# Expert layers: the second block's remainder of the down weights is subtracted on GpSimd instead of VectorE

## The chip, the cores and the metric

The kernel runs on one core of a Trainium2 chip. The metric is the device time of one execution in microseconds. The time before is the median of 3 runs; one more execution was taken with the hardware profiler.

## What is computed

One inference step of a small diffusion backbone with two layers over 640 tokens (512 latent, 128 context), model width 1024. Each layer has an attention mixer (differential attention in layer 0, latent attention in layer 1) and then the channel mixer with which this change deals: PEER, a retrieval among 16384 experts, of which each token and head takes 16.

```
def peer(h, wq, sub_keys, u, v):        # per block xb of 128 tokens
    q = (xb @ wq).reshape(TOK_BLOCK, PEER_HEADS, 2, PEER_HALF)
    s = einsum('thcd,hcnd->thcn', q, sub_keys)
    top_s, top_i = lax.top_k(s, PEER_TOPK)
    ...
    g = jax.nn.softmax(fs, axis=-1)
    ue = u[idx]
    a = jax.nn.gelu(einsum('td,thkd->thk', xb, ue))
    ve = v[idx]
    return einsum('thk,thkd->td', g * a, ve)
```

`u` and `v` are the up and down weights, 16384 x 1024 f32 each per layer.

## The kernel before

The program is one instruction stream per engine with semaphores set by hand. In each layer, after the attention, `expert_choice` finds the experts of each token ("choice stage") and builds a dense table of gates ("gate stage"). `experts` then applies them in two ways at the same time ("expert stage"). For the first three token blocks (TD = 384 tokens) all experts are computed densely on TensorE, with the gates, mostly zero, multiplied in. For the other two token blocks the rows of the chosen experts are gathered from DRAM and worked through on VectorE.

**Dense part.** The experts come in N = 64 blocks `i` of NE = 2 times 128 (`k` = 0, 1). f32 precision is reached with operands that are split in a rounded part (`h`) and its remainder (`l`), both of type fp32r; a product is the sum of three: h·h, h·l, l·h.
- SyncE (SP) loads u (1 MB), v (1 MB) and, every other block, the gates (768 KB) two blocks ahead; raw u and v are double-buffered in `rawu` and `rawv` (slices of `ring`). A load waits until the remainder of the block that used the buffer is made.
- ScalarE rounds: `round_u(i + 1, k)` (L1803), `round_v(i, k)` (L1810), `gelu` (L1816), `round_w` (L1822), `row_gelu` (L1826).
- VectorE makes the remainders by a subtraction, raw minus rounded: `rest_u` (L1870), `rest_v` (L1875), `rest_w` (L1887), and multiplies the gates in, `gate` (L1882). `Us`, `Vs` hold one block's pair; there is only one buffer for each.
- TensorE does `up(i + 1)` (L1743, 48 products of 384 columns) and then `down(i)` (L1765, 36 products of 512 columns); `down(i)` waits per `k` for the remainders of the gated activations (`wl`) and of v (`vl`).

**Gathered part.** 256 gathers per layer (`m`), each 128 rows of 8 KB (u and v side by side) into one of GSLOTS = 6 slots. GpSimd issues gather m when `acc` says that row m - 6 is used up. VectorE does `dots` (L1896, a product with the token and its sum), ScalarE the gelu, VectorE `accs` (L1902 and L1911, times v and added). Two rows (a pair n) belong to each (i, k), four to each block.

The order of VectorE's work in a block is written out by hand: for k = 0, 1: `dots`, `gate(i, k)`, `rest_u(i + 1, k)`, `accs`, `rest_w(i, k)`; then `rest_v(i, 0)`, `rest_v(i, 1)`. At gather rows 128 and 256 (blocks 31 and 63) two partial sums are added (L1915).

Outside of the expert stage GpSimd also does two-input operations: in the choice stage it multiplies and adds tables (L1500, L1503, L1505) while VectorE works on the next token block; there VectorE's two-input instructions are L1534 and L1595, among searches with one input.

Of the kernel before, what the change touches and what calls it, by code (L numbers as in the profile page):

```python
# [17 lines left out]
F32 = mybir.dt.float32  # L18
# [3 lines left out]
ALU = mybir.AluOpType  # L22
# [4 lines left out]
D = 1024  # L27
# [13 lines left out]
NE = 2  # L41
# [19 lines left out]
def mixed(nc, cst, inp, outs, g_dram, x_dram):  # L61
# [3 lines left out]
    def sem(name):  # L65
        if name not in sems:
            sems[name] = es.enter_context(nc.semaphore(name))
        return sems[name]
# [25 lines left out]
    def bank2(b, n=T, p=P):  # L94

        return ps[0:p, b:b + 2, :].rearrange("p a n -> p (a n)")[:, 0:n]
# [1579 lines left out]
    def experts(l, rows, gates, hs, ht, Us, Vs, Gt, rawu, rawv, Ws, gbuf, act4):  # L1676

        n_ = "ex_"
        N = P // NE
# [10 lines left out]
        def up_bank(k):  # L1690
            return ps[:, 6 + k, 0:TD]

        with nc.Block() as block:
            @block.sync
            def _(sp):
                for q in range(2):
                    sp.wait_ge(sem(f"gm_out{q}"), 16 * 8)
                for i in range(N):
                    s = i % 2
                    if i >= 2:  # L1700
                        sp.wait_ge(sem(n_ + "ul"), NE * (i - 1))
                        sp.dma_start(rawu[:, s, :], inp["u"][l, i]).then_inc(sem(n_ + f"u_in{s}"), 16)
                    if i % 2 == 0:
                        g = i // 2
                        if g >= 2:
                            sp.wait_ge(sem(n_ + "gc"), 2 * (g - 1))
                        sp.dma_start(Gt[:, g % 2, :, :].rearrange("p t k -> p (t k)"),
                                     g_dram[g].rearrange("p t k -> p (t k)")).then_inc(sem(n_ + f"g_in{g % 2}"), 16)
                    if i >= 2:
                        sp.wait_ge(sem(n_ + "vl"), NE * (i - 1))  # L1710
                    sp.dma_start(rawv[:, s, :], inp["v"][l, i]).then_inc(sem(n_ + f"v_in{s}"), 16)
                sp.wait_ge(sem(n_ + "acc"), NI - 2)
                sp.wait_ge(sem(n_ + "wg"), NE * (N - 1))
                sp.dma_start(xT[:], x_dram).then_inc(sem("x_back"), 16)
                if l == 1:
                    for j in range(4):
                        sp.wait_ge(sem(n_ + "x"), 4 * (j + 1))
                        sp.dma_start(outs["y"][:, 2 * j:2 * j + 2], xT[:, 2 * j:2 * j + 2]).then_inc(sem("stored"), 16)

            @block.gpsimd  # L1720
            def _(pool):
                for m in range(NI):
                    b, j = divmod(m, P)
                    if m >= GSLOTS:
                        pool.wait_ge(sem(n_ + "acc"), m - GSLOTS + 1)
                    c = b * P + j
                    pool.indirect_dma_start(out=slots[m % GSLOTS], out_offset=None, in_=inp[f"uv{l}"],  # L1727
                                            in_offset=bass.IndirectOffsetOnAxis(ap=rows[:, c:c + 1], axis=0))\
                        .then_inc(sem(f"row_in{m % GSLOTS}"), 16)

            @block.tensor
            def _(pe):
                def up(i):

                    for k in range(NE):
                        pe.wait_ge(sem(n_ + "ul"), NE * i + k + 1)
                        if i >= 1:
                            pe.wait_ge(sem(n_ + "gelu"), NE * (i - 1) + k + 1)
                        for dc in range(DC):
                            if i + k == 0:  # L1740
                                pe.wait_ge(sem(n_ + "hl"), dc + 1)
                            for x, y in ((0, 0), (0, 1), (1, 0)):
                                mm = pe.matmul(up_bank(k), Us[x][:, k, dc * P:(dc + 1) * P], hs[y][:, dc, :],  # L1743
                                               start=dc == 0 and x + y == 0, stop=dc == DC - 1 and x == 1)
                        mm.then_inc(sem(n_ + "a"), 1)

                def down(i):

                    for k in range(NE):
                        pe.wait_ge(sem(n_ + "wl"), NE * i + k + 1)  # L1750
                        pe.wait_ge(sem(n_ + "vl"), NE * i + k + 1)
                        if i + k == 0:
                            pe.wait_ge(sem(n_ + "htc"), 2)
                        if (i, k) == (N - 1, NE - 1):
                            for tb in range(3):
                                for x, y in ((0, 0), (1, 0), (0, 1)):
                                    for half in range(2):
                                        mm = pe.matmul(ps[:, 2 * tb + half, :], Ws[i % 2][x][:, k, tb * P:(tb + 1) * P],  # L1758
                                                       Vs[y][:, k, half * 512:(half + 1) * 512], start=False, stop=y == 1)
                                mm.then_inc(sem(n_ + "y"), 1)  # L1760
                            continue
                        for x, y in ((0, 0), (1, 0), (0, 1)):
                            for tb in range(3):
                                for half in range(2):
                                    mm = pe.matmul(ps[:, 2 * tb + half, :], Ws[i % 2][x][:, k, tb * P:(tb + 1) * P],  # L1765
                                                   Vs[y][:, k, half * 512:(half + 1) * 512],
                                                   start=i == 0 and k == 0 and x + y == 0,
                                                   stop=False)
                        mm.then_inc(sem(n_ + "y"), 1)

                for b in range(2):
                    for dc in range(DC):
                        mm = pe.transpose(ps[:, 2 * b + dc // 4, (dc % 4) * P:(dc % 4 + 1) * P],
                                          hT[:, dc, GB[b] * P:(GB[b] + 1) * P], ident)
                    mm.then_inc(sem(n_ + "ht"), 1)
                up(0)
                for i in range(N):
                    if i + 1 < N:
                        up(i + 1)
                    down(i)  # L1780

                for b in range(2):
                    pe.wait_ge(sem(n_ + "ysum"), b + 1)
                pe.wait_ge(sem(n_ + "gelu"), NE * N)
                for dc in range(DC):
                    if dc >= 4:
                        pe.wait_ge(sem(n_ + "x"), 2 * (dc - 3))
                    out = bank2(2 * ((dc + 3) % 4))
                    for tb in (3, 4, 0, 1, 2):
                        if dc == 0 and tb < 3:  # L1790
                            pe.wait_ge(sem(n_ + "yc"), tb + 1)
                        src = (Yd[tb] if tb < 3 else Yb[tb - 3])[:, dc * P:(dc + 1) * P]
                        mm = pe.transpose(out[:, tb * P:(tb + 1) * P], src, ident)
                    mm.then_inc(sem(n_ + "yt"), 1)
# [72 lines left out]
            def _(v):  # L1867
                def rest_u(i, k):
                    v.wait_ge(sem(n_ + "uh"), NE * i + k + 1)
                    v.tensor_tensor(Us[1][:, k, :], rawu[:, i % 2, k * D:(k + 1) * D], Us[0][:, k, :].bitcast(F32),  # L1870
                                    ALU.subtract).then_inc(sem(n_ + "ul"), 1)

                def rest_v(i, k):
                    v.wait_ge(sem(n_ + "vh"), NE * i + k + 1)
                    v.tensor_tensor(Vs[1][:, k, :], rawv[:, i % 2, k * D:(k + 1) * D], Vs[0][:, k, :].bitcast(F32),  # L1875
                                    ALU.subtract).then_inc(sem(n_ + "vl"), 1)

                def gate(i, k):
# [47 lines left out]
                for i in range(N):  # L1926
                    if i == 0:
                        for k in range(NE):
                            dots(k)
                            rest_u(1, k)  # L1930
                    for k in range(NE):
                        if i:
                            dots(2 * i + k)
                        gate(i, k)
                        if i and i + 1 < N:
                            rest_u(i + 1, k)
                        accs(2 * i + k)
                        rest_w(i, k)
                    for k in range(NE):
                        rest_v(i, k)  # L1940
                v.wait_ge(sem("x_back"), 16 * (l + 1))
                for dc in range(DC):
                    v.wait_ge(sem(n_ + "yt"), dc + 1)
# [240 lines left out]
```

## Time and profile before

| | |
|---|---|
| median of 3 runs | 3924.34 us (3922.66 to 3928.52) |
| profiled execution | 3924.41 us, span 3922.6 us |
| granted TensorE clock, mean | 0.965 |
| busy: PE, DVE, ACT, POOL | 95%, 83%, 45%, 28% of the span |
| HBM | 970.69 MB read, 59.39 MB written |

PE is TensorE, DVE VectorE, ACT ScalarE, POOL GpSimd, SP SyncE with its DMA queue. Busy shares are averages over the whole span. A granted clock of 1.00 is TensorE's full 2.4 GHz.

### The profile page before, as it was taken

What the parts mean: (1) busy time and instruction counts of PE and PEld (TensorE: products, weight loads), DVE (VectorE), ACT (ScalarE), POOL (GpSimd) and SP (SyncE); (2) the same over time, 40 slices, a digit from 0 to 9 for tenths busy, and PEclk for the clock granted to TensorE, in tenths of its full rate; (3) what the DMA queues carried; (4) which work ended last, traced back from release to release, by engine and by line L of the source; (5) the groups of instructions that cost most, each with busy time, mean ns of one, the idle gap of its engine ahead of it and who ended that gap; (6) DMA issues with size and microseconds to landing.
All of it is one profiled execution on the core that took longest, in us unless ns stands there. A gap on an engine that the chain in (4) does not pass through costs nothing. (4 is left out here: it accounts for less than half of the span.)

```text
span 3922.6 us, 55734 instructions
## 1 busy us (share of the span) xinstructions
PE 3731.2 (95%) x20637; PEld 3146.4 (80%) x20637; DVE 3239.0 (83%) x6793; ACT 1758.5 (45%) x2888; POOL 1117.1 (28%) x836
## 2 busy tenths in 40 slices
PE   8999999888999999999989999996899999999999
PEld 4546789688999999999854646896889999999998
DVE  5737639898999999999963636399899999999998
ACT  3315522394444444444423646223944444444443
POOL 0000003493333333333200000035833333333332
PEclk9999889799999999999989999897999999999999
DMA  7310030299999999999841010301999999999997
GB/s 300 140 43 12 22 128 2 108 251 409 421 413 408 405 406 404 404 405 406 326 175 52 1 43 22 128 2 51 266 426 418 413 409 404 404 406 403 406 405 296
DMA packets 268270, 1033.70 MB, mean 264 GB/s; under 512 B 147072, under 2 KB 150080, under 8 KB 159936
## 3 DMA queue, kind: packets, MB, share of 16 engines
q0 software_dynamic: 77184, 562.07, 35.7%
q1 hardware_dynamic: 190816, 468.07, 31.4%
q8 instruction: 165, 2.70, 0.3%
q14 instruction: 105, 0.86, 0.1%
HBM read 970.69 MB, written 59.39 MB: 263 GB/s over the span
## 5 line engine op out<-in xcount | busy, mean ns | idle before, releaser
L1727 POOL DMA_INDIRECT gbuf<-in_uv,rows x340 | 514.8, 1514 | 863.6 <-DVE hT L1911 793.8
L1911 DVE SCALAR_TENSOR_TENSOR hT<-gbuf,act,hT 128x1024 f32<-128x1024 f32 x336 | 416.9, 1282 | 6.0
L1896 DVE SCALAR_TENSOR_TENSOR gbuf<-gbuf,ht 128x1024 f32<-128x1024 f32 x340 | 402.0, 1219 | 11.5 <-DMA gbuf<-in_uv,rows 11.5
L1727 POOL DMA_INDIRECT xT<-in_uv,rows x172 | 256.9, 1494 | 473.0 <-DVE hT L1911 393.2
L1500 POOL TENSOR_TENSOR eq<-eq,tabs 128x4096 f16<-128x4096 f16 x8 | 63.5, 7940 | 1070.2 <-DVE eq L1550 981.3
L1743 PE MATMUL ps<-h0h,U0h 128*128 128x384 f32 x1024 | 345.0, 337 | 6.8 <-DVE U0l L1870 6.8
L1743 PE MATMUL ps<-h1h,U1h 128*128 128x384 f32 x1024 | 345.2, 337 | 6.0 <-DVE U1l L1870 6.0
L1743 PE MATMUL ps<-h1h,U1l 128*128 128x384 f32 x1024 | 344.5, 336 | 0.0
L1743 PE MATMUL ps<-h0h,U0l 128*128 128x384 f32 x1024 | 344.4, 336 | 0.0
L1743 PE MATMUL ps<-h1l,U1h 128*128 128x384 f32 x1024 | 344.3, 336 | 0.0
L1743 PE MATMUL ps<-h0l,U0h 128*128 128x384 f32 x1024 | 344.2, 336 | 0.0
L1816 ACT ACTIVATE ring<-ps 128x384 f32<-128x384 f32 x256 | 125.9, 492 | 392.4 <-PE ps L1743 392.3
L1826 ACT ACTIVATE act<-act 128x2 f32<-128x2 f32 x256 | 51.8, 202 | 444.7 <-DVE gbuf L1896 296.4
L1336 PE MATMUL ps<-hT,ring 128*128 128x128 f32 x1920 | 232.5, 281 | 6.1 <-ACT hT L317 4.5
L1336 PEld LDWEIGHTS ps<-hT,ring 128*128 128x128 f32 x1920 | 225.1, 196 | 10.8 <-ACT hT L317 5.7
L1388 PE MATMUL ps<-pqT,w 128*128 128x128 f32 x1536 | 190.6, 282 | 37.2 <-DVE w L1651 32.3
L1388 PEld LDWEIGHTS ps<-pqT,w 128*128 128x128 f32 x1536 | 180.5, 196 | 47.7 <-DVE w L1651 28.0
L1512 POOL TENSOR_SCALAR pqT<-iota,selT 128x128 f32<-128x128 f32 x256 | 203.8, 810 | 51.1 <-ACT selT L1443 28.4
L1896 DVE SCALAR_TENSOR_TENSOR xT<-xT,ht 128x1024 f32<-128x1024 f32 x172 | 203.5, 1220 | 9.6 <-DMA xT<-in_uv,rows 9.6
L1911 DVE SCALAR_TENSOR_TENSOR hT<-xT,act,hT 128x1024 f32<-128x1024 f32 x168 | 208.4, 1282 | 3.0
L1743 PEld LDWEIGHTS ps<-h0h,U0h 128*128 128x128 f32 x1024 | 193.5, 189 | 10.0 <-DVE U0l L1870 7.5
L1743 PEld LDWEIGHTS ps<-h1h,U1h 128*128 128x128 f32 x1024 | 193.9, 189 | 9.1 <-DVE U1l L1870 6.6
(392 smaller groups left out, 9150.3 us busy)
## 6 DMA issues: line engine op xcount, KB each, us to landing
ring<-in_u SPq DMA_DIRECT2D x128, 1024.0 KB, 12.5
ring<-in_v SPq DMA_DIRECT2D x128, 1024.0 KB
ring<-in_wts SPq DMA_DIRECT2D x26, 2048.0 KB, 8.8
gates<-ring SPq DMA_DIRECT2D x32, 1536.0 KB, 7.3
ring<-gates SPq DMA_DIRECT2D x64, 768.0 KB
abuf<-in_ada_mid POOLq DMA_DIRECT2D x16, 1024.0 KB, 5.1
xT<-in_ada_late SPq DMA_DIRECT2D x16, 1024.0 KB, 4.9
abuf_c<-in_ada_late POOLq DMA_DIRECT2D x8, 1024.0 KB, 5.1
```

The costliest lines, as they stand in the source:

```text
L1336: mm = pe.matmul(ps[:, 5 + n % 3, q * P:(q + 1) * P], w[:, dc, q * P:(q + 1) * P], hT[:, dc, tb * P:(tb + 1) * P], start=dc == 0, stop=dc ...
L1388: mm = pe.matmul(ps[:, b + t // 4, (t % 4) * P:(t % 4 + 1) * P], one1[:, r % 2, t, :], one2[:, r % 2, t, :], start=True, stop=True)
L1500: pool.tensor_tensor(eq4, eq4, tab4, ALU.mult).then_inc(look, 1)
L1512: last = pool.tensor_scalar(one2[:, r % 2, t, :], iota[:], selT[:, 1, t0 + t:t0 + t + 1], selT[:, 2, t0 + t:t0 + t + 1], ALU.is_equal, ALU ...
L1727: pool.indirect_dma_start(out=slots[m % GSLOTS], out_offset=None, in_=inp[f"uv{l}"], in_offset=bass.IndirectOffsetOnAxis(ap=rows[:, c:c + ...
L1743: mm = pe.matmul(up_bank(k), Us[x][:, k, dc * P:(dc + 1) * P], hs[y][:, dc, :], start=dc == 0 and x + y == 0, stop=dc == DC - 1 and x == 1)
L1816: act.activation(Wf[:, k, :], up_bank(k), ACT.Gelu_apprx_tanh).then_inc(sem(n_ + "gelu"), 1)
L1826: act.activation(act4[:, n % 2, 0:2], act4[:, n % 2, 0:2], ACT.Gelu_apprx_tanh)\
L1896: v.scalar_tensor_tensor(u, u, 1.0, ht[:, m // P, :], ALU.mult, ALU.mult, accum_out=act4[:, n % 2, m % 2:m % 2 + 1]).then_inc(sem(n_ + "do ...
L1911: v.scalar_tensor_tensor(y, x, w, y, ALU.mult, ALU.add).then_inc(sem(n_ + "acc"), 1)
```

## The change

In the expert stage the remainder for k = 1 is no longer made by VectorE but by GpSimd, between two gathers; k = 0 stays with VectorE. GpSimd signals on a semaphore of its own, `vp`; TensorE's `down(i, 1)` waits for `vp` in place of `vl`, and the load of v two blocks later waits for both. In GpSimd's stream the subtraction of block i stands behind gather m = 4i + 9, and the last two behind the last gather.

```diff
                     if i >= 2:
-                        sp.wait_ge(sem(n_ + "vl"), NE * (i - 1))
+                        sp.wait_ge(sem(n_ + "vl"), i - 1)
+                        sp.wait_ge(sem(n_ + "vp"), i - 1)
                     sp.dma_start(rawv[:, s, :], inp["v"][l, i]).then_inc(sem(n_ + f"v_in{s}"), 16)
...
             @block.gpsimd
             def _(pool):
+                def rest_v(i):
+
+                    pool.wait_ge(sem(n_ + "vh"), NE * (i + 1))
+                    pool.tensor_tensor(Vs[1][:, 1, :], rawv[:, i % 2, D:2 * D], Vs[0][:, 1, :].bitcast(F32), ALU.subtract)\
+                        .then_inc(sem(n_ + "vp"), 1)
+
                 for m in range(NI):
...
+                    if m >= 9 and m % 4 == 1:
+                        rest_v(m // 4 - 2)
+                rest_v(N - 2)
+                rest_v(N - 1)
...
-                        pe.wait_ge(sem(n_ + "vl"), NE * i + k + 1)
+                        pe.wait_ge(sem(n_ + ("vl", "vp")[k]), i + 1)
...
-                def rest_v(i, k):
-                    v.wait_ge(sem(n_ + "vh"), NE * i + k + 1)
-                    v.tensor_tensor(Vs[1][:, k, :], rawv[:, i % 2, k * D:(k + 1) * D], Vs[0][:, k, :].bitcast(F32),
+                def rest_v(i):
+                    v.wait_ge(sem(n_ + "vh"), NE * i + 1)
+                    v.tensor_tensor(Vs[1][:, 0, :], rawv[:, i % 2, 0:D], Vs[0][:, 0, :].bitcast(F32),
                                     ALU.subtract).then_inc(sem(n_ + "vl"), 1)
...
-                    for k in range(NE):
-                        rest_v(i, k)
+                    rest_v(i)
```

## Rows read from the trace of the kernel before

**Rows 1.** The page: busy shares of the engines, chain that ended last by line

```profile
PE 3731.2 (95%) x20637; PEld 3146.4 (80%) x20637; DVE 3239.0 (83%) x6793; ACT 1758.5 (45%) x2888; POOL 1117.1 (28%) x836
...
PE ps L1765 13%; PE ps L1743 13%; DMA gbuf<-in_uv,rows 0%; DVE hT L1911 0%; DVE xT L1945 0%; DVE gbuf L1896 0%; PE ps L1758 0%; DVE V1l L1875 0%; DVE U1l L1870 0%; DVE xT L1896 0%; POOL xT L1727 0%; DVE W01l L1887 0%; DVE ring L1882 0%; DVE hT L1915 0%; POOL gbuf L1727 0%
```

**Rows 2.** Windows of layer 0, gate and expert stage: length, busy us, clock, DMA

```profile
core 0: us, PE busy (x) PEld busy (x) DVE busy (x) ACT busy (x) POOL busy (x), PEclk, DMA share, GB/s
785.00:880.00 95.00, 86.59 (x714) 81.91 (x715) 92.92 (x117) 91.95 (x203) 90.58 (x117) 1.00 1.00 252
...
1200.00:1900.00 700.00, 700.00 (x3553) 638.48 (x3552) 685.35 (x934) 320.97 (x466) 258.23 (x170) 1.00 1.00 405
```

**Rows 3.** The chain in order of time: start us, us, what

```profile
2892.03 8.34 PE ps L1743 x48
2908.58 8.35 PE ps L1743 x48
```

**Rows 4.** Timeline of VectorE, layer 1, rest_v of blocks 0 and 17

```profile
2865.73 2.35 DVE L1875 TENSOR_TENSOR V1l<-ring,V1h 128x1024 fp32r<-128x1024 f32 x2
...
3140.67 2.35 DVE L1875 TENSOR_TENSOR V1l<-ring,V1h 128x1024 fp32r<-128x1024 f32 x2
```

**Rows 5.** Timeline of VectorE, layer 0, from one block's end to the next's

```profile
1391.03 2.35 DVE L1875 TENSOR_TENSOR V0l<-ring,V0h 128x1024 fp32r<-128x1024 f32 x2
...
1407.57 2.35 DVE L1875 TENSOR_TENSOR V0l<-ring,V0h 128x1024 fp32r<-128x1024 f32 x2
1409.84 1.22 DVE L1896 SCALAR_TENSOR_TENSOR gbuf<-gbuf,ht 128x1024 f32<-128x1024 f32 x1
...
1412.97 1.23 DVE L1870 TENSOR_TENSOR U0l<-ring,U0h 128x1024 fp32r<-128x1024 f32 x1 [0.29 <-ACT U0h L1803]
```

**Rows 6.** Timeline of VectorE and TensorE, last block of layer 1

```profile
3898.67 1.23 DVE L1915 TENSOR_TENSOR hT<-hT 128x1024 f32<-128x1024 f32 x1
...
3900.40 1.22 DVE L1875 TENSOR_TENSOR V1l<-ring,V1h 128x1024 fp32r<-128x1024 f32 x1
...
3901.77 1.61 PE L1765 MATMUL ps<-V1h,W11h 128*128 128x512 f32 x6 [0.40 <-DVE V1l L1875]
```

**Rows 7.** Groups of GpSimd by form, 619 to 705 us: busy us, mean ns

```profile
L1503 POOL TENSOR_TENSOR eq<-eq 128x1024 f16<-128x1024 f16 x3 | 6.4, 2125 | 0.2
L1503 POOL TENSOR_TENSOR eq<-eq 128x512 f16<-128x512 f16 x3 | 3.5, 1152 | 0.2
```

**Rows 8.** Timeline of GpSimd, layer 0: the second gather of a pair, then the next pair

```profile
1408.30 1.30 POOL L1727 DMA_INDIRECT gbuf<-in_uv,rows  x1 [0.30 <-issue]
1415.86 1.74 POOL L1727 DMA_INDIRECT gbuf<-in_uv,rows  x1 [6.26 <-DVE hT L1911]
```

**Rows 9.** Timeline of VectorE without and with GpSimd beside it; GpSimd's two groups there

```profile
607.40 0.89 DVE L1595 TENSOR_TENSOR cand<-vals 128x128 f32<-128x128 f32 x4
607.60 0.55 DVE L1595 TENSOR_TENSOR cand<-vals 128x192 f32<-128x192 f32 x2
...
739.73 2.44 DVE L1534 TENSOR_TENSOR gates<-fs,small 128x128 f32<-128x128 f32 x1
742.30 3.76 DVE L1595 TENSOR_TENSOR cand<-vals 128x128 f32<-128x128 f32 x4
744.42 1.50 DVE L1595 TENSOR_TENSOR cand<-vals 128x192 f32<-128x192 f32 x2
...
737.96 7.81 POOL L1503 TENSOR_TENSOR eq<-eq 128x2048 f16<-128x2048 f16 x3
...
L1503 POOL TENSOR_TENSOR eq<-eq 128x2048 f16<-128x2048 f16 x1 | 4.1, 4052 | 0.1
...
L1503 POOL TENSOR_TENSOR eq<-eq 128x1024 f16<-128x1024 f16 x1 | 2.2, 2249 | 0.1
...
744.42 1.35 POOL L1503 TENSOR_TENSOR eq<-eq 128x512 f16<-128x512 f16 x1
```

**Rows 10.** The u loads: issue on SP, the cast that follows, issue to landing

```profile
1410.32 0.43 SPq L1702 DMA_DIRECT2D ring<-in_u  x1
...
1411.89 1.04 ACT L1803 CAST U0h<-ring 128x1024 fp32r<-128x1024 f32 x1
...
DMA to landing us min/median/max: 8.9/12.6/22.1
```

## The prediction

> **What bounds the kernel now.** I started from the page's busy shares and the chain that ended last [rows 1]: TensorE is busy 95% of the span, and the chain is the matmuls of L1743 (up) and L1765 (down). VectorE, at 83%, looks as if it had room. That share is an average over stages, so I went to the windows of the expert stage [rows 2]. There TensorE is busy 100% of the time at a granted clock of 1.00 (the 2.4 GHz level), and VectorE 97.9% (685.35 of 700), with DMA at 1.00: two engines are full, and one of them only just follows the other. The chain [rows 3] gives TensorE's pace: up products start every 16.55 us (2892.03 to 2908.58). The timeline of VectorE gives the other pace. The remainders of a block's down weights start at 2865.73, and 17 blocks later at 3140.67 [rows 4]: 274.94 / 17 = 16.17 us (16.173) a block, with no wait between. Later the step is 16.54 (1391.03 to 1407.57), because VectorE has caught up and waits 0.29 us in each block for ScalarE's rounded up weights [rows 5], which themselves follow a product of TensorE. So TensorE is the bound with 16.55, and VectorE is behind it by only 0.38 us a block. At the last block both are critical: VectorE comes from the sum at 3898.67 to rest_v at 3900.40 without a gap, and TensorE waits 0.40 for it [rows 6].
>
> How much room does VectorE have in a layer? From the first rest_v (2865.73) to that of the last block (3900.40) are 63 steps in 1034.67 us. Without waits they would be 62 x 16.173 = 1002.7, plus 1.23 for the sum of the two halves at block 31 (L1915, as at 3898.67), plus a last step of 16.17 - 2 x 1.14 (no rest_u, each as long as a rest_v) + 1.23 = 15.12. Together 1019.1: **15.6 us of room a layer**, 0.25 us for each of 63 blocks. More than that per block and the layer gets longer, by all of the excess.
>
> **The change, part by part.**
>
> VectorE loses one rest_v a block. The pair starts at 1407.57 and the next instruction at 1409.84 [rows 5], so one takes 1.135 us: -1.135 a block. By itself that is worth nothing, since TensorE's chain stays: only the 0.40 us at a layer's end.
>
> GpSimd gets one two-input operation of 128x1024 f32 a block. The nearest rows are its two-input operations in the choice stage: 128x1024 f16 took 2125 ns and 128x512 took 1152 ns where VectorE did only one-input work beside them [rows 7]. GpSimd has time: it issues its gathers in pairs of 1.74 + 0.30 + 1.30 us, two a block, and idles 6.26 us before the next pair [rows 8]. The operation comes behind the second gather of the pair that the end of the block releases (1408.30 + 1.30 = 1409.60), so it would start near 1409.7 and end near 1412, and the next pair is due at 1415.86. So no gather is late.
>
> What it costs is elsewhere. Look at VectorE in the choice stage while GpSimd works on two inputs [rows 9]: four small additions (L1595) that take 0.89 us together at 607.40 take 3.76 at 742.30, and one product (L1534) of 128x128 takes 2.44. The ends line up with GpSimd's: the product ends at 739.73 + 2.44 = 742.17, and the operation of GpSimd that ran beside it (4052 ns, from 737.96) at 742.02. Operations with one input went on at their usual speed. So a VectorE instruction with two inputs from SBUF stands still while GpSimd reads two. The Trainium skill says the same: SBUF — State Buffer, section "Who interferes with whom", has an exclusive lock on a shared port pair, and a VectorE instruction with two SBUF inputs contends with a GpSimd instruction that reads SBUF. The trace agrees: 3.76 us against 0.89. By that rule the sum is the one below; by busy times alone (VectorE minus 1.135) it would be zero.
>
> In the expert loop every VectorE instruction but the 0.08 us accumulator reads has two SBUF inputs (dots, gate, rest_u, accs, rest_w). So what GpSimd holds, VectorE loses; nothing covers it. How long is a hold? A 128x512 operation of GpSimd started at 744.42 beside a VectorE pair (128x192, 128x128) that took 1.50; the same pair takes 0.55 free, at 607.60. The stall is 1.50 - 0.55 = 0.95, against the 1152 ns that GpSimd's operation takes alone: 0.20 less, since GpSimd's dispatch and VectorE's own start overlap the other's work. It also shows that GpSimd gets in between two queued VectorE instructions. For 1024 elements that makes 2.125 - 0.20 = 1.92. The upper bound is the whole of a stretched 128x1024 operation, 2.25 (2249 ns). The rows are f16 inputs, the new operation has f32; no row shows two f32 inputs on GpSimd. I take the middle, **2.08 us**, and keep 1.92 and 2.25. The Trainium skill (GPSIMD Engine Reference, section "Performance versus the Vector engine") has 4497 ns for a two-input f32 addition of 2048 elements; half of it less 0.20 would be an estimated 2.05 and the time about 4008. No run here shows it.
>
> VectorE then needs 16.17 - 1.135 + 2.08 = 17.12 a block, above TensorE's 16.55: it becomes the bound. Per layer: 63 x (2.08 - 1.135) = 59.5, less the room of 15.6 = 43.9. Two layers: +87.8 us.
>
> The waits that change cost less. TensorE's down(i, 1) now waits for GpSimd. It is due half a down later than down(i, 0): (16.55 - 8.34) / 2 = 4.1 us [rows 3]. That follows VectorE's rest_v(i, 0), so 1407.57 + 1.22 + 4.1 = 1412.9. If GpSimd takes the port at 1409.9 it is done near 1412.0; if a dots goes first (1.15), near 1413.1. Then TensorE waits some 0.3, and has 17.12 - 16.55 = 0.57 to spare: 0. GpSimd's own wait for ScalarE's rounding is over when it comes: VectorE starts on the second half at 1408.70 today, before 1409.6. The load of v now also waits for GpSimd, and behind it in SP's queue stand the loads of u and of the gates. The u load moves from 1410.32 to about 1412.5; the cast that reads it comes a block after that at 1411.89, near 1429, so some 16.5 us stay, against landings of 12.6 in the middle and 22.1 at most [rows 10]. The traffic per us is 3% thinner then. I put 0 here, at most 10 us. TensorE's clock: in the gate stage it is busy 86.6 of 95 us at a granted clock of 1.00 [rows 2], so idling 3% should not lower it: 0.
>
> **Sum.** The profiled execution took 3924.4 us (span 3922.6), 0.1 us from the median of the runs. 3924.4 + 87.8 = **4012 us**. With a hold of 1.92: 63 x 0.785 - 15.6 = 33.9 a layer, 3992. With 2.25: 54.6 a layer, 4034. The chances take 0.2% (8 us) as what a measurement can tell from no change.
>
> **Rivals.**
> - *The hold is short or the port is shared.* If GpSimd holds VectorE less than 1.135 + 0.25 = 1.385 us a block, TensorE stays the bound: 3924, at best 3923 with the 0.40 at each layer's end. For it: the operation could run beside instructions with long streams, which the small ones of the choice stage don't show. Against it: VectorE's instructions stood still to the end of GpSimd's in [rows 9]. Chance 0.08. This is the case that is not slower. A gain over 8 us has nothing to come from, since TensorE has no waits in the stage: 0.02.
> - *Partly shared*, hold 1.4 to 1.65: 3926 to 3957. Chance 0.05.
> - *GpSimd is held out.* If VectorE's stream keeps it from the port over 4.1 us (beyond the 6.26 us of idle before the next pair, less 2.1), the gathers are issued late, and VectorE waits for rows. At 1 us a block that is 126 us more, about 4140. Against it: GpSimd got in behind one queued instruction at 744.4. Chance 0.05, and 0.03 for an f32 operation of well over 2.4 us.
> - *The forecast*, hold 1.7 to 2.4 and VectorE the bound: 0.77.
>
> **Numbers.** The forecast's own range comes from holds of 1.7 and 2.4 us: 3924.4 + 2 x (63 x 0.565 - 15.6) = 3964, and 3924.4 + 2 x (63 x 1.265 - 15.6) = 4053. That holds 0.77, and with a margin of a few us at both ends 0.8: 3960 to 4055. Slower by over 0.2%: 0.77 + 0.08 + 0.05 = 0.90; the same 0.08; faster 0.02.
>
> **What would show it.** In the expert windows TensorE's busy time falls to about 97%, and VectorE's rises to 99% or more. The step between rest_v starts is 17.1 us from the first block on, and TensorE waits for VectorE's remainders of u (L1870), about 0.57 us a block. One dots of the four in a block takes about 3.2 us instead of 1.22, so the mean of L1896 rises to about 1.7. GpSimd's subtraction takes 2.1 to 3.4 us with the wait in it. Wrong: dots at 1.22 while GpSimd subtracts (no lock); steps of 16.55 (hold under 1.385); VectorE idle before L1896 on a DMA (late gathers), or before L1870 on ScalarE behind a u load (late loads).

## The result, and the profile after

The changed kernel takes 4032.6 us (median of 4 runs, 4029.37 to 4036.52) against 3925.3 us in the same runs of the kernel before: ratio 1.027, 95% interval 1.0254 to 1.0287. It is slower by 107 us; the forecast was 4012, 88 us slower. The profiled execution's span is 4031.3 us against 3922.6, 108.7 us more.

The page of the changed kernel: busy shares, and the chain that ended last by line. The lines of the code have moved: dots are now L1907 (L1896 before), accs L1922 (L1911), rest_u L1881 (L1870), rest_v on VectorE L1886 (L1875), up L1754 (L1743), down L1776 (L1765).

```profile
PE 3777.4 (94%) x20637; PEld 3143.2 (78%) x20637; DVE 3366.3 (84%) x6665; ACT 1743.5 (43%) x2888; POOL 1444.2 (36%) x964
...
DVE 22%; issue 5%; DMA 0%; PE 0%; POOL 0%; DVEq 0%; ACT 0%; POOLq 0%
```

In [rows 1] the chain was made of matmuls. Now it is VectorE, and TensorE's share is 0%. VectorE's busy time has risen by 127 us although it has 128 instructions fewer. The window of the expert stage, which answers to [rows 2]:

```profile
1200.00:1900.00 700.00, 685.18 (x3412) 611.48 (x3411) 697.06 (x855) 305.27 (x448) 349.81 (x203) 1.00 0.98 389
```

TensorE is down from 100% to 97.9%, VectorE up from 97.9% to 99.6%, the granted clock still 1.00 (the 2.4 GHz level). Now the timeline of VectorE, one block; it answers to [rows 5].

```profile
1468.84 1.22 DVE L1886 TENSOR_TENSOR V0l<-ring,V0h 128x1024 fp32r<-128x1024 f32 x1
1469.98 1.22 DVE L1907 SCALAR_TENSOR_TENSOR xT<-xT,ht 128x1024 f32<-128x1024 f32 x1
...
1471.12 3.42 DVE L1907 SCALAR_TENSOR_TENSOR xT<-xT,ht 128x1024 f32<-128x1024 f32 x1
...
1474.47 0.55 DVE L1893 TENSOR_TENSOR ring<-ring,hT 128x384 f32<-128x384 f32 x1
...
1486.08 1.22 DVE L1886 TENSOR_TENSOR V0l<-ring,V0h 128x1024 fp32r<-128x1024 f32 x1
```

And GpSimd beside it, in its timeline:

```profile
1469.57 1.30 POOL L1734 DMA_INDIRECT gbuf<-in_uv,rows  x1 [0.31 <-issue]
1470.89 2.56 POOL L1726 TENSOR_TENSOR V0l<-ring,V0h 128x1024 fp32r<-128x1024 f32 x1
```

The durations of its subtractions in layer 0, in ns (min, median, max):

```profile
L1726 POOL TENSOR_TENSOR V0l<-ring,V0h x64: 2341/2561/3440, 918.8 to 2000.4; 128x1024 fp32r<-128x1024 f32 x64
```

The first dots of the block takes its 1.22 us. The second starts at 1471.12, during GpSimd's subtraction, and takes 3.42: it ends at 1474.54, which is 1.09 us after GpSimd's end at 1473.45, so it did all its work afterwards. The stall is 3.42 - 1.22 = 2.20 us. The step from rest_v to rest_v is 1486.08 - 1468.84 = 17.24 us, against the 16.55 of before.

### The profile page after: what moved, and what is told of

It reads as the page before. It is cut to its first block and busy times, and to the rows that moved or that the text cites. A ratio compares the mean times of both kernels' runs of the same rounds, so it can differ in the third digit from the quotient of the medians.

```text
span 4031.3 us, 55859 instructions
## 1 busy us (share of the span) xinstructions
PE 3777.4 (94%) x20637; PEld 3143.2 (78%) x20637; DVE 3366.3 (84%) x6665; ACT 1743.5 (43%) x2888; POOL 1444.2 (36%) x964
## 5 line engine op out<-in xcount | busy, mean ns | idle before, releaser
L1907 DVE SCALAR_TENSOR_TENSOR gbuf<-gbuf,ht 128x1024 f32<-128x1024 f32 x340 | 581.9, 1748 | 11.5 <-DMA gbuf<-in_uv,rows 11.5
L1922 DVE SCALAR_TENSOR_TENSOR hT<-gbuf,act,hT 128x1024 f32<-128x1024 f32 x336 | 416.9, 1282 | 6.0
L1754 PE MATMUL ps<-h0h,U0h 128*128 128x384 f32 x1024 | 351.5, 343 | 24.6 <-DVE U0l L1881 24.6
L1754 PE MATMUL ps<-h1h,U1h 128*128 128x384 f32 x1024 | 351.9, 344 | 23.8 <-DVE U1l L1881 23.8
L1754 PE MATMUL ps<-h0h,U0l 128*128 128x384 f32 x1024 | 345.9, 338 | 0.0
L1754 PE MATMUL ps<-h1h,U1l 128*128 128x384 f32 x1024 | 345.7, 338 | 0.0
L1754 PE MATMUL ps<-h1l,U1h 128*128 128x384 f32 x1024 | 345.1, 337 | 0.0
L1754 PE MATMUL ps<-h0l,U0h 128*128 128x384 f32 x1024 | 345.1, 337 | 0.0
L1907 DVE SCALAR_TENSOR_TENSOR xT<-xT,ht 128x1024 f32<-128x1024 f32 x172 | 282.4, 1679 | 9.8 <-DMA xT<-in_uv,rows 9.8
L1754 PEld LDWEIGHTS ps<-h0h,U0h 128*128 128x128 f32 x1024 | 193.8, 189 | 45.0 <-DVE U0l L1881 42.5
L1754 PEld LDWEIGHTS ps<-h1h,U1h 128*128 128x128 f32 x1024 | 193.9, 189 | 44.3 <-DVE U1l L1881 41.8
L1922 DVE SCALAR_TENSOR_TENSOR hT<-xT,act,hT 128x1024 f32<-128x1024 f32 x168 | 208.4, 1282 | 3.0
L101 PE MATMUL ps<-hT,ring 128*128 128x512 f32 (+1 forms) x368 | 194.9, 612 | 5.0 <-ACT hT L317 5.0
```

The lines of the kernel that those rows point to most:

```text
L101: e.matmul(out[:, 0:512], lhsT, rhs[:, 0:512], start=start, stop=stop)
L1907: v.scalar_tensor_tensor(u, u, 1.0, ht[:, m // P, :], ALU.mult, ALU.mult, accum_out=act4[:, n % 2, m % 2:m % 2 + 1]).then_inc(sem(n_ + "do ...
L1922: v.scalar_tensor_tensor(y, x, w, y, ALU.mult, ALU.add).then_inc(sem(n_ + "acc"), 1)
```

## The experiments

All of them are edits of the changed kernel, except the one that says otherwise. In this section B is the time of the kernel before on the same chip, and **stall** is what the stretched VectorE instruction takes beyond its usual time. The forecast's formula, with what a block adds to VectorE's 16.17 us as d, is B + 2 x (63 d - 15.6) where that is above B. The table compares it with what was measured, d taken from each trace.

| run | d, from its trace | formula | measured (median) | ratio, 95% interval |
|---|---|---|---|---|
| the change | 2.20 - 1.14 = 1.06 | +102 | +107 | 1.0254 to 1.0287 |
| e1_left_out | -1.14 | 0 | +0.9 | 0.9993 to 1.0013 |
| e2_memset | -1.14 | 0 | +0.7 | 0.9988 to 1.0007 |
| e3_half | 1.49 - 0.54 = 0.95 | +89 | +95 | 1.0223 to 1.0258 |
| e4_twice | 19.37 - 16.17 = 3.20 | +372 | +388 | one run |
| e5_copy | 0.83 - 1.14 = -0.31 | 0 | +1.4 | 0.9994 to 1.0014 |
| e6_one_input | 15.93 - 16.17 = -0.24 | 0 | +1.3 | 0.9995 to 1.0014 |
| e7_f16 | 1.69 - 1.14 = 0.55 | +38 | +44 | 1.0097 to 1.0131 |
| e8_ahead | 2.21 - 1.14 = 1.07 | +104 | +110 | 1.0259 to 1.0294 |
| e9_half_ahead | 1.10 - 0.54 = 0.56 | +39 | +39 | 1.0089 to 1.0122 |
| e10_dve_extra | 1.26 | +128 | +125 | 1.0312 to 1.0347 |
| e11_every_second | 1.06 in every second block | +37 | +38 | 1.0083 to 1.0117 |

**Without the subtraction (e1).** Where the changed kernel waits for GpSimd, TensorE and the load of v wait for ScalarE's rounding instead.

```diff
-                    pool.tensor_tensor(Vs[1][:, 1, :], rawv[:, i % 2, D:2 * D], ...
-                    if m >= 9 and m % 4 == 1:
-                        rest_v(m // 4 - 2)
...
-                        pe.wait_ge(sem(n_ + ("vl", "vp")[k]), i + 1)
+                        pe.wait_ge(sem(n_ + ("vl", "vh")[k]), (i + 1, NE * (i + 1))[k])
...
-                                                   Vs[y][:, k, half * 512:(half + 1) * 512],
+                                                   Vs[y * (1 - k)][:, k, half * 512:(half + 1) * 512],
```

> Leaves the remainder of the second block's down weights out on both engines (TensorE uses the rounded half in its place and waits for ScalarE's rounding); nothing else changes. Theory (GpSimd's hold of the port is the whole loss): VectorE has 15.04 us of work a block, TensorE's 16.55 bounds, 3924 us, the step is 16.55 and the dots stay at 1.22. Rival (the loss comes from the reordered waits of TensorE and SP): also near 3925, so this run only shows what taking the work off VectorE is worth; more than 8 us below 3925 would show that VectorE's load had cost TensorE something.

3925.7 us against 3924.8. Window of the expert stage:

```profile
1200.00:1900.00 700.00, 700.00 (x3552) 638.43 (x3551) 641.29 (x892) 320.67 (x466) 256.96 (x170) 1.00 1.00 405
```

VectorE is busy 91.6% instead of 97.9%, and nothing is gained: TensorE was busy 100% and is again. So the work that the change takes off VectorE was worth nothing even had GpSimd been free of charge.

**A fill in the place of the subtraction (e2).**

```diff
-                    pool.tensor_tensor(Vs[1][:, 1, :], rawv[:, i % 2, D:2 * D], Vs[0][:, 1, :].bitcast(F32), ALU.subtract)\
-                        .then_inc(sem(n_ + "vp"), 1)
+                    pool.memset(Vs[1][:, 1, :].bitcast(F32), 0.0).then_inc(sem(n_ + "vp"), 1)
```

> GpSimd fills the second block's remainder with zeros at the same place, with the same waits and signals, and reads nothing. Theory (only reads of GpSimd block VectorE's second input): dots 1.22, step 16.55, 3925 us. Rival A (the waits on GpSimd and its place between the gathers cost the time): 4033. Rival B (every access of GpSimd blocks, writes too): the dots beside the fill are stretched by its length, some 1 us; below 1.385 us a block, so the time is again 3925, and only the dots tell it apart.

3925.5 us. Groups of VectorE and GpSimd by form, expert stage of layer 0:

```profile
L1906 DVE SCALAR_TENSOR_TENSOR gbuf<-gbuf,ht 128x1024 f32<-128x1024 f32 x152 | 179.9, 1220 | 1.7 <-DMA gbuf<-in_uv,rows 1.7
...
L1726 POOL MEMSET V0l<- 128x1024 f32 x57 | 55.5, 973 | 0.0
```

The dots keep their 1220 ns beside fills of 973 ns. In the whole run no dots takes more than 1226 ns. The waits, the signals and the place in GpSimd's queue are those of the changed kernel, and they cost nothing: rivals A and B fall. A signal that comes as late as the real subtraction's isn't tested by a fill of 0.97 us; e6 does that. What costs is that GpSimd reads.

**Half of it (e3).** GpSimd takes columns 512 to 1023, VectorE the first 512.

```diff
-                    pool.tensor_tensor(Vs[1][:, 1, :], rawv[:, i % 2, D:2 * D], Vs[0][:, 1, :].bitcast(F32), ALU.subtract)\
+                    pool.tensor_tensor(Vs[1][:, 1, H:D], rawv[:, i % 2, D + H:2 * D], Vs[0][:, 1, H:D].bitcast(F32), ALU.subtract)\
...
+                    v.wait_ge(sem(n_ + "vh"), NE * (i + 1))
+                    v.tensor_tensor(Vs[1][:, 1, 0:H], rawv[:, i % 2, D:D + H], Vs[0][:, 1, 0:H].bitcast(F32),
+                                    ALU.subtract).then_inc(sem(n_ + "vl"), 1)
```

> GpSimd subtracts only columns 512 to 1023 of the second block's remainder, VectorE the first 512. Theory (a hold in proportion to the elements): hold about 1.1 us for 512 f32 columns, VectorE saves 0.53 a block and loses 1.1, +0.57 against 0.25 of room: 3925 + 126 x 0.32 = 3966 us, step 16.75. Rival A (f32 holds no longer than the 0.95 us of the f16 rows): +0.42, 3946. Rival B (a hold of fixed length per instruction, 2.2 us): +1.67, 4104.

4020.2 us, a miss by 54 us: neither the theory nor rival A. Timelines of VectorE and GpSimd:

```profile
1466.27 0.69 DVE L1892 TENSOR_TENSOR V0l<-ring,V0h 128x512 fp32r<-128x512 f32 x1
1466.87 2.71 DVE L1913 SCALAR_TENSOR_TENSOR xT<-xT,ht 128x1024 f32<-128x1024 f32 x1
...
1465.86 1.30 POOL L1735 DMA_INDIRECT gbuf<-in_uv,rows  x1 [0.30 <-issue]
1467.18 1.30 POOL L1727 TENSOR_TENSOR V0l<-ring,V0h 128x512 fp32r<-128x512 f32 x1
```

GpSimd's half takes 1.30 us, but the stall is 2.71 - 1.22 = 1.49. The dots started at 1466.87, 0.31 us before GpSimd's recorded start, and yet it ended 1.10 us after GpSimd's end (1468.48), so it had done nothing before. It looks as if GpSimd had the port already while it worked on the gather in front. e9 tests that.

**Twice (e4).** The same subtraction again, behind a wait for the first.

```diff
+                    pool.tensor_tensor(Vs[1][:, 1, :], rawv[:, i % 2, D:2 * D], Vs[0][:, 1, :].bitcast(F32), ALU.subtract)\
+                        .then_inc(sem(n_ + "vp"), 1)
+                    pool.wait_ge(sem(n_ + "vp"), 2 * i + 1)
                     pool.tensor_tensor(Vs[1][:, 1, :], ...
```

> GpSimd does the same subtraction twice, one behind the other with a wait between, the same output. Theory: two holds of 2.2 us a block, step 17.23 + 2.2 = 19.43, 4033 + 126 x 2.2 = 4310 us. Rival (the loss is a late wait or a one-time shift, and GpSimd has 4.4 us idle a block to take the second in): 4033 to 4050.

4313 us, against 4310 expected. Two VectorE instructions a block are stretched, the second dots to 3.41 and the gate behind it from 0.55 to 2.68:

```profile
1461.74 3.41 DVE L1910 SCALAR_TENSOR_TENSOR gbuf<-gbuf,ht 128x1024 f32<-128x1024 f32 x1
...
1465.09 2.68 DVE L1896 TENSOR_TENSOR ring<-ring,hT 128x384 f32<-128x384 f32 x1
```

That GpSimd has the idle time to take the second one in doesn't help: the price is paid by VectorE. The formula is 16 us short here. About 9 us of it lie within the layers: the 63 steps of layer 1 took 1225.0 us against 1034.7, 190.3 more where the formula has 186, since a layer's 128 subtractions all fall within 63 steps, two more than the formula counts. The rest, some 8 us, lies behind the layers, 6 of it between the two, and I have not traced it; the granted clock of the first 57 us there (2143 to 2200 us) is 0.71, against 0.76 in the kernel before (from 1953.6 us). In the expert window the granted clock is 0.97, because it falls for short stretches behind waits of TensorE (0.68 from 1236 to 1239 us), but VectorE's step stays 19.37, so that costs nothing there.

**One input on GpSimd (e5).**

```diff
-                    pool.tensor_tensor(Vs[1][:, 1, :], rawv[:, i % 2, D:2 * D], ...
+                    pool.tensor_copy(Vs[1][:, 1, :], rawv[:, i % 2, D:2 * D]).then_inc(sem(n_ + "vp"), 1)
```

> GpSimd copies the raw second half of the down weights into the remainder's place instead of subtracting: the same output size, place, waits and signals, but one input (so the remainder is wrong by its size). Theory (any GpSimd read of SBUF blocks VectorE's two-input instructions for as long as it lasts): the copy takes some 1.1 us, one dots a block stretched by 1.1 to 1.4; against the 1.385 us that GpSimd may hold, 3925 to 3935 us, step 16.55. Rival (only a two-input operation of GpSimd blocks): dots at 1.22 everywhere, 3925.

3925.8 us. Timelines of VectorE and GpSimd:

```profile
1474.47 1.22 DVE L1906 SCALAR_TENSOR_TENSOR gbuf<-gbuf,ht 128x1024 f32<-128x1024 f32 x1
...
1475.61 2.05 DVE L1906 SCALAR_TENSOR_TENSOR gbuf<-gbuf,ht 128x1024 f32<-128x1024 f32 x1
...
1475.37 1.22 POOL L1726 CAST V0l<-ring 128x1024 fp32r<-128x1024 f32 x1
```

One dots a block is stretched, by 2.05 - 1.22 = 0.83 us. A one-input read blocks too, only for a shorter time, less than the 1.385 us that VectorE can lose here, so the total doesn't show it. The rival falls; the theory's 1.1 to 1.4 was too long.

**One input on VectorE (e6).**

```diff
-                        v.scalar_tensor_tensor(u, u, 1.0, ht[:, m // P, :], ALU.mult, ALU.mult,
-                                               accum_out=act4[:, n % 2, m % 2:m % 2 + 1]).then_inc(sem(n_ + "dot"), 1)
+                        v.tensor_scalar(u, u, 1.0, 0.0, ALU.mult, ALU.add,
+                                        accum_out=act4[:, n % 2, m % 2:m % 2 + 1]).then_inc(sem(n_ + "dot"), 1)
```

> The changed kernel, but the dots of VectorE have one input (the row times 1.0, summed; the product with the token is left out). GpSimd's subtraction starts beside them. Theory (only VectorE instructions with two SBUF inputs are blocked): dots stay at 1.2; the subtraction runs past them and stretches the gate behind them by about 1 us; 15.04 + 1 = 16.0 a block, TensorE bounds with 16.55, 3925 us. Rival (GpSimd blocks whatever VectorE does, or its late signal is the cost): 4033.

3925.8 us. GpSimd's subtraction is there in every block (2.41 us), and TensorE bounds again. Timeline of VectorE, then of GpSimd, layer 0, of the early blocks in which VectorE doesn't wait for anything:

```profile
1010.36 1.22 DVE L1886 TENSOR_TENSOR V0l<-ring,V0h 128x1024 fp32r<-128x1024 f32 x1
...
1013.77 1.47 DVE L1893 TENSOR_TENSOR ring<-ring,hT 128x384 f32<-128x384 f32 x1
...
1026.29 1.22 DVE L1886 TENSOR_TENSOR V0l<-ring,V0h 128x1024 fp32r<-128x1024 f32 x1
...
1012.41 2.41 POOL L1726 TENSOR_TENSOR V0l<-ring,V0h 128x1024 fp32r<-128x1024 f32 x1
```

The dots keep 1.21 us each (groups by form: 1212 and 1211 ns) while GpSimd subtracts beside them. The gate, the next instruction with two inputs, starts at 1013.77 and ends at 1015.24, again just after GpSimd's end at 1014.82: 0.92 us of stall. The step is 15.93. So GpSimd's subtraction leaves dots with one input alone and stops the gate with two, and the 107 us are gone when the work beside GpSimd is of the first kind. The 2.41 us subtraction with its late signal costs nothing by itself either. Other kinds of VectorE instructions with one input were not tried.

**f16 inputs (e7).** They are the gather indices read as f16, minus themselves; the remainder is zero.

```diff
-                    pool.tensor_tensor(Vs[1][:, 1, :], rawv[:, i % 2, D:2 * D], ...
+                    a = rows[:, 0:2 * P].bitcast(F16).unsqueeze(1).to_broadcast([P, 2, 4 * P])
+                    pool.tensor_tensor(Vs[1][:, 1, :].rearrange("p (a n) -> p a n", a=2), a, a, ALU.subtract)\
```

> GpSimd's subtraction reads two f16 inputs of 1024 elements (the gather indices seen as f16, minus themselves, so the remainder is zero) instead of f32. Theory (the forecast's hold was too small because f32 inputs take longer on GpSimd than the f16 rows: 2.34 against 2.125 us alone): hold 2.0 instead of 2.2, step 17.02, 4033 - 126 x 0.215 = 4006 us. Rival (the element type makes no difference, the excess is elsewhere): step 17.23, 4033.

3968.8 us: more than the theory's gain, and not the rival's none. Durations in layer 0 (min, median, max):

```profile
L1727 POOL TENSOR_TENSOR V0l<-rows x64: 1893/2057/2940, 918.0 to 1967.6; 128x1024 fp32r<-128x1024 f16 x64
```

A stretched dots in VectorE's timeline:

```profile
1470.88 2.91 DVE L1908 SCALAR_TENSOR_TENSOR gbuf<-gbuf,ht 128x1024 f32<-128x1024 f32 x1
```

With f16 inputs the operation takes 1.89 us undisturbed and stalls VectorE for 1.69; with f32 it takes 2.34 and stalls it for 2.20. The difference of 0.45 us is that of the element type, as far as this run can tell it: the edit also makes both inputs the same 512 elements, read twice, and I have not separated the two. Nor is the 2.125 of [rows 7] a price that goes by element type and count alone: that operation adds two strided halves of a table and writes f16, and the one here takes 1.89 us.

**In front of the gathers (e8).**

```diff
+                    if m >= 8 and m % 4 == 0:
+                        rest_v(m // 4 - 2)
                     if m >= GSLOTS:
                         pool.wait_ge(sem(n_ + "acc"), m - GSLOTS + 1)
...
-                    if m >= 9 and m % 4 == 1:
-                        rest_v(m // 4 - 2)
```

> GpSimd's subtraction stands in front of the pair of gathers that a block's end releases instead of behind it. Theory (the hold costs VectorE the same wherever it falls, give or take the 0.3 us that the place within a VectorE instruction makes): step 17.1 to 17.5, 4015 to 4070 us, another VectorE instruction stretched (accs, rest_w or rest_v). Rival (the cost comes from its place between the gathers and the dots): near 3925. Rival B (gathers issued 2.5 us later make VectorE wait for rows): above 4070.

4034.8 us, as the change itself. Timeline of VectorE:

```profile
1468.04 2.76 DVE L1898 TENSOR_TENSOR W00l<-ring,W00h 128x384 fp32r<-128x384 f32 x1
```

The durations of GpSimd's subtractions in layer 0:

```profile
L1726 POOL TENSOR_TENSOR V0l<-ring,V0h x64: 2338/3456/3467, 915.9 to 2000.4; 128x1024 fp32r<-128x1024 f32 x64
```

Now rest_w is the instruction that stands still, from 0.55 to 2.76, 2.21 us. The subtraction itself takes 3.46 us, because it has to wait through a whole accs first; VectorE doesn't pay for that. Rival and rival B fall: the place doesn't matter, nor do gathers issued 2.5 us later.

**Half, in front of the gathers (e9).** The edits of e3 and e8 together.

> The half subtraction of 512 columns, in front of the pair of gathers, where GpSimd has waited for ScalarE just before it. Theory (behind a gather GpSimd takes the port already before its recorded start, as soon as VectorE ends an instruction, so that the stall of 1.49 us in the half subtraction holds some 0.3 us in which GpSimd still works on the gather; behind an idle wait it takes it no earlier than its start): stall about 1.1 us, step 15.04 + 0.60 + 1.10 = 16.74, 3925 + 126 x (1.70 - 1.135 - 0.25) = 3965 us. Rival (a hold has a fixed part of 0.6 us whatever stands before it): step 17.13, 4020 as in the half subtraction.

3968.1 us, 52 us faster than the same half behind the gathers. Timelines of VectorE and GpSimd:

```profile
1467.83 1.65 DVE L1904 TENSOR_TENSOR W10l<-ring,W10h 128x384 fp32r<-128x384 f32 x1
...
1466.72 2.34 POOL L1727 TENSOR_TENSOR V0l<-ring,V0h 128x512 fp32r<-128x512 f32 x1 [3.35 <-ACT V0h L1824]
```

The stall is 1.65 - 0.55 = 1.10 us here and 1.49 behind a gather. The hold has no fixed part of 0.6; its length depends on what GpSimd did just before and on where VectorE's instruction ends.

**More work for VectorE alone (e10).** An edit of the kernel before: VectorE makes the remainder of the first half twice.

```diff
+                    v.wait_ge(sem(n_ + "vh"), NE * i + 1)
+                    v.tensor_tensor(Vs[1][:, 0, :], rawv[:, i % 2, 0:D], Vs[0][:, 0, :].bitcast(F32), ALU.subtract)\
+                     .then_inc(sem(n_ + "vx"), 1)
+                    v.wait_ge(sem(n_ + "vx"), i + 1)
                     for k in range(NE):
                         rest_v(i, k)
```

> The kernel before, with VectorE making the remainder of the first half twice (with a wait between, the same output): 1.14 to 1.20 us more of VectorE work a block, and nothing on GpSimd. Theory (VectorE has 15.6 us of room in a layer, and all beyond it lengthens the layer): step 17.3 to 17.37, 63 x 1.17 - 15.6 = 58 a layer, 3925 + 116 + 3 = 4044 us. Rival (part of the changed kernel's loss needs GpSimd or the changed waits, so VectorE's load alone costs less): under 4020.

4053.5 us. Timeline of VectorE:

```profile
1473.55 1.22 DVE L1940 TENSOR_TENSOR V0l<-ring,V0h 128x1024 fp32r<-128x1024 f32 x1
1474.80 2.36 DVE L1875 TENSOR_TENSOR V0l<-ring,V0h 128x1024 fp32r<-128x1024 f32 x2
```

The extra instruction costs 1.25 us with its wait, a little more than I had put in; the formula with 1.26 (a step of 17.43) gives +128, measured +125. This is the changed kernel's loss without GpSimd: VectorE's room is as small as the forecast said, and the rival (under 4020) falls.

**Every second block (e11).** GpSimd subtracts in the odd blocks only.

```diff
                 def rest_v(i):
+                    if i % 2 == 0:
+                        return
...
+                    if i % 2 == 0:
+                        v.wait_ge(sem(n_ + "vh"), NE * i + 2)
+                        v.tensor_tensor(Vs[1][:, 1, :], rawv[:, i % 2, D:2 * D], ...
```

> GpSimd subtracts only in the odd blocks; in the even ones VectorE makes both remainders as before. Theory (a stall of 2.2 less the 1.135 saved per moved remainder, against 15.6 us of room a layer): 32 x 1.06 - 15.6 = 18.3 a layer, 3925 + 37 + up to 4 at the ends = 3962 to 3966 us. Rival (the loss comes with any use, in proportion to it): half of the full change's 107, 3979. Rival B (the room takes it all): 3925.

3967.1 us, +38, and the steps alternate between 16.17 and 17.23 us. Half the moves cost a third of the whole, as the formula has it, which takes the room off first. The rivals (3979 and 3925) fall.

## Why the prediction was right, and where it was off

- **VectorE becomes the bound.** Right. The step is 17.23 instead of the forecast's 17.12, from the first blocks on, and the chain is VectorE's. TensorE waits for the remainders of u before L1754, 48 us in all by the page. That is 0.38 us a block where I had said 0.57; the rest of the longer step stands in the profile as busy time, 46 us more of it (3777.4 against 3731.2) for the same 20637 instructions.
- **A two-input instruction of VectorE stands still while GpSimd reads.** Right, and shown from both sides: a fill that doesn't read costs nothing (e2), dots with one input aren't touched (e6), a second subtraction costs nearly the same again (e4: 2.13 us on the gate), and another place moves the stall to another instruction at the same price (e8). The lock of the Trainium skill (SBUF — State Buffer, "Who interferes with whom") agrees in all of them, down to the one-input read of e5.
- **One is taken off, -1.135, worth nothing alone.** Right: e1.
- **The room of 15.6 us a layer.** Right within 1 us. In e10, where VectorE has no room left, the 63 steps took 1097.7 us; less 63 x 1.257 they are 1018.5, against 1019.1 in the forecast, so the room is 16.2. The 1.23 for the sum at block 31 is largely given back, which I had left out: soon behind it the first `accs` of the second half have one input less, and the two take 1.42 us instead of 2.48 (timeline of VectorE in the changed kernel):

```profile
1460.09 1.42 DVE L1919 TENSOR_SCALAR hT<-gbuf,act 128x1024 f32<-128x1024 f32 x2
```

- **The hold of 2.08 us.** This is the term that was mis-sized. It measured 2.20 (17.23 - 15.04 = 2.19 by the step). I took it from f16 rows; with f32 inputs the operation takes 2.34 us alone, above both of my row prices for it. 0.115 us x 126 = 14.5 us of the 20.9 by which the span's growth of 108.7 exceeds the forecast's 87.8. The estimates from the Trainium skill's 4497 ns for twice the elements (GPSIMD Engine Reference, "Performance versus the Vector engine") were 2.05 for the hold and 2.25 for the operation; the measurement, 2.20 and 2.34, is above both.
- **The clock costs nothing.** Right within the stage (window 1.00), wrong at a layer's end. TensorE waits 7.82 us there for the last rest_v, and then the first twelve products of down are slow. Timeline of TensorE in the changed kernel:

```profile
4008.49 2.90 PE L1776 MATMUL ps<-V1h,W11h 128*128 128x512 f32 x6 [7.82 <-DVE V1l L1886]
4011.19 2.15 PE L1776 MATMUL ps<-V1h,W11l 128*128 128x512 f32 x6
```

  and the window around it, in the columns of [rows 2]:

```profile
4000.00:4016.00 16.00, 8.19 (x28) 6.27 (x28) 8.24 (x9) 2.61 (x4) 2.34 (x1) 0.79 0.31 134
```

  The same six took 1.61 in [rows 6]. The granted clock is 0.79 in these 16 us, part of them at the lower level of 1.2 GHz. From the last rest_v to the end of the kernel are 24.2 us against 22.2 before: 2 us. Between the layers it is 2 us as well (915.4 against 913.4 us from the last rest_v of layer 0 to the first of layer 1), and 0.9 us come back because the first rest_v of all starts that much earlier: 3.1 us together.
- **The rest.** From the first rest_v to that of the last block are 1087.5 us in layer 1 against 1034.7, 52.8 more, where 63 x 1.06 - 15.6 is 51.2. About 1.6 us a layer are left, and they have three parts. My sum counted a hold for each of the 63 steps, but all 64 subtractions of a layer fall within them (918.8 to 2000.4 us in layer 0, the steps 916.8 to 2004.3): one more stall. That is the last one, +2.1: it stretches the sum at block 63 from 1.23 to 3.31 us, just before the last rest_v (timelines of GpSimd and VectorE):

```profile
2000.37 2.34 POOL L1726 TENSOR_TENSOR V0l<-ring,V0h 128x1024 fp32r<-128x1024 f32 x1 [12.65 <-ACT V0h L1821]
...
2000.48 3.31 DVE L1926 TENSOR_TENSOR hT<-hT 128x1024 f32<-128x1024 f32 x1
```

  At block 31 the subtraction meets rest_v and not a dots (below), +0.3. The room, 16.2 and not 15.6, takes off 0.6. Together that is 1.8, within the rounding of the 1.06. Over both layers the 1.6 measured make 3.2, and 14.5 + 3.2 + 3.1 make the 20.8.
- **Late signal, late loads.** Right at 0: TensorE waits 0.8 us in all for GpSimd, ScalarE 2.6 us in layer 1 for loads of u.
- **The rivals.** The short and the shared hold fell with the 2.20 us. (The upper end of the shared one should have been 3958, not 3957.) GpSimd was not held out: its longest subtraction took 3.45 us, of which some 1.1 are waiting, and VectorE's waits for gathered rows before the dots are 21.3 us in all against 21.1 before.

## What to carry to other kernels

Before work moves to GpSimd, count what VectorE does beside it: if those are instructions with two SBUF inputs, what VectorE loses is nearly the length of GpSimd's operation, here 2.20 us for an operation of 2.34, with 1.14 saved, and GpSimd's idle time is no measure of the price. A balanced pair of engines has little room (0.25 us a block of 16.55 here), so compute the follower's free step from a stretch in which it doesn't wait before you add or remove anything. An operation that only writes, or has one input, is the one to give away: the fill cost VectorE nothing and the copy 0.83 us.

## What the runs showed of the hardware that I had not expected

**The port can be taken before the recorded start.** In e3 a dots that had started 0.31 us before GpSimd's operation still waited for all of it, where GpSimd came straight from a gather. In the changed kernel itself it happens at block 31 (timelines of VectorE and GpSimd):

```profile
1452.33 3.76 DVE L1886 TENSOR_TENSOR V0l<-ring,V0h 128x1024 fp32r<-128x1024 f32 x1
...
1451.67 0.95 POOL L1734 DMA_INDIRECT xT<-in_uv,rows  x1 [0.30 <-issue]
1452.65 2.35 POOL L1726 TENSOR_TENSOR V0l<-ring,V0h 128x1024 fp32r<-128x1024 f32 x1
```

rest_v starts 0.32 us earlier and stalls for 3.76 - 1.22 = 2.54 us, longer than the whole operation. A dots that had started 0.91 us earlier (1469.98 against 1470.89) was not blocked; it was GpSimd that waited. Where GpSimd came from an idle wait (e8, e9), the operation began 0.1 us after an accs and had to wait through it. So behind a gather the port seems to be claimed somewhere between 0.3 and 0.9 us ahead of the recorded start. Whether it is the gather or the next operation that claims it is not settled. The one run with a subtraction behind another operation is e4, where the second comes behind the first and a wait: it starts at 1464.15, 0.08 us after the first has ended at 1464.07, and takes 3.20 us: the dots that had stood still goes first.

**GpSimd's prices by input.** For 1024 columns undisturbed: 0.96 us to fill, 1.04 to copy f32, 1.89 to subtract f16 from f16 (with the inputs of e7), 2.34 to subtract f32 from f32; 1.26 for 512 columns of f32.
